# Attention scores: norms beside the up projections, paired score products, padded rotated rows

## The reference, cut to what matters

```python
q_nope = rms_norm(q[..., :128], mla_q_g[:128])          # 4 heads, 192 = 128 + 64
q_pe   = apply_rope(rms_norm(q[..., 128:], mla_q_g[128:]), cos, sin)
k_nope = rms_norm(kv[..., :128], mla_k_g[:128])
k_pe   = apply_rope(rms_norm(kpe_raw, mla_k_g[128:]), cos, sin)   # one, shared by the heads
out_m  = causal_attention(([q_nope, q_pe],), ([k_nope, k_pe],), (1.0,), v_m, 192 ** -0.5)
# differential attention: 4 heads with two score matrices of 64 features each
out_d  = causal_attention((qd0, qd1), (kd0, kd1), (1.0, -lam), vd, 64 ** -0.5)
# causal_attention: scores + causal mask, softmax, (sum_i c_i p_i) @ v, per block of 128 queries
```

## Time and profile before

| what | us |
|---|---|
| median of three runs | 3252.24 |
| span of the profiled execution, first to last instruction | 3238.1 |
| median less span (start and end of a run, and another execution) | 14.1 |
| PE busy, share of the span | 3122.7, 96% |
| DVE busy | 2023.3, 62% |
| ACT busy | 1268.4, 39% |
| POOL busy | 788.4, 24% |
| attention steps 0 to 14 (first score product to the MLA transposes) | 70.5 |
| MLA transposes | 5.7 |
| steps 15 to 35 | 46.8 |

### The profile page before, as it was taken

One profiled execution on the slowest core, in us unless ns is written; L12 is line 12 of the kernel. 1 busy time (PEld: TensorE's weight loads), 2 busy tenths in 40 slices (PEclk: granted clock), 3 DMA queues, 4 the chain that ended last, 5 costly groups with the idle time before them and its releaser, 6 DMA issues.

```text
span 3238.1 us, 42699 instructions
## 1 busy us (share of the span) xinstructions
PE 3122.7 (96%) x16801; PEld 2703.6 (83%) x16801; DVE 2023.3 (62%) x3671; ACT 1268.4 (39%) x2154; POOL 788.4 (24%) x513
## 2 busy tenths in 40 slices
PE   8999999989999999999998989999999997999999
PEld 6769989878888888888786678999999996888887
DVE  5576565663232464333458555989879767787877
ACT  6364443343232434322334332335444453333332
POOL 1000010100000020000002100686776764343452
PEclk9999999989999999999998899999999998999999
DMA  4303221233332323333231022578888889999997
GB/s 126 105 29 104 60 68 51 72 110 99 98 98 97 115 94 91 92 99 97 83 96 47 1 66 79 180 268 294 295 283 328 280 313 360 349 347 343 335 344 267
DMA packets 234375, 539.36 MB, mean 167 GB/s; under 512 B 24816, under 2 KB 91632, under 8 KB 231104
## 3 DMA queue, kind: packets, MB, share of 16 engines
q1 hardware_dynamic: 196736, 400.27, 37.5%
q0 software_dynamic: 37440, 136.36, 11.5%
HBM read 484.10 MB, written 52.46 MB: 166 GB/s over the span
## 4 chain that ended last, share of the span: by engine, by line
PE 76%; DVE 12%; DMA 6%; ACT 2%; POOL 2%; issue 1%; SPq 0%; DVEq 0%; ACTq 0%
PE bank L382 22%; PE bank L385 15%; PE bank L2349 11%; PE bank L2780 9%; DMA gl<-acts 4%; PE bank L2508 3%; PE bank L1109 2%; PE bank L1119 2%; PE bank L1070 2%; PE bank L1058 2%; PE bank L1923 1%; DVE vsl L2827 1%; DMA eu<-in_peer_u 1%; POOL etl L2337 1%; PE bank L505 1%
## 5 line engine op out<-in xcount | busy, mean ns | idle before, releaser
L332 DVE TENSOR_TENSOR wl<-raw,wh 128x1024 fp32r<-128x1024 f32 (+2 forms) x241 | 296.7, 1234 | 644.4 <-ACT wh L317 644.2
L317 ACT CAST wh<-raw 128x1024 fp32r<-128x1024 f32 (+2 forms) x241 | 249.7, 1038 | 655.8 <-PE bank L382 367.2
L2337 POOL TENSOR_TENSOR etl<-eu,eth 128x1024 fp32r<-128x1024 f32 x128 | 319.5, 2498 | 410.3 <-ACT eth L2333 408.9
L2349 PE MATMUL bank<-peerhh,eth 128*128 128x384 f32 x1024 | 349.6, 341 | 14.7 <-POOL etl L2337 12.6
L2349 PE MATMUL bank<-peerhl,eth 128*128 128x384 f32 x1024 | 344.0, 336 | 0.0
L2349 PE MATMUL bank<-peerhh,etl 128*128 128x384 f32 x1024 | 343.8, 336 | 0.0
L2780 PE MATMUL bank<-vsh,coefh 128*128 128x512 f32 x768 | 300.5, 391 | 19.2 <-DVE coefl L2847 19.2
L2374 POOL DMA_INDIRECT taken<-in_peer_v,gb x128 | 228.0, 1782 | 299.3 <-DVE y_row L2394 292.8
L2780 PE MATMUL bank<-vsh,coefl 128*128 128x512 f32 x768 | 299.8, 390 | 0.0
L2780 PE MATMUL bank<-vsl,coefh 128*128 128x512 f32 x768 | 299.8, 390 | 0.0
L2333 ACT CAST eth<-eu 128x1024 fp32r<-128x1024 f32 x128 | 135.7, 1061 | 200.1 <-DMA eu<-in_peer_u 195.5
(11 more groups left out here) (568 smaller groups left out, 7363.5 us busy)
## 6 DMA issues: line engine op xcount, KB each, us to landing
eu<-in_peer_u SPq DMA_DIRECT2D x128, 512.0 KB
vb<-in_peer_v SPq DMA_DIRECT2D x128, 512.0 KB, 5.6
raw<-in_ada_w SPq DMA_DIRECT2D x48, 512.0 KB, 3.8
acts<-eg SPq DMA_DIRECT2D x128, 192.0 KB
coefs<-stage SPq DMA_DIRECT2D x24, 1024.0 KB
gd<-coefs SPq DMA_DIRECT2D x16, 1536.0 KB, 12.9
gl<-acts SPq DMA_DIRECT2D x128, 192.0 KB
raw<-in_ffn_w_gate SPq DMA_DIRECT2D x44, 512.0 KB, 3.6
```

The source lines that it names most:

```text
L317: act.copy(parts_of(c)[0], raw_of(c)).then_inc(*up("w rounded", c))
L332: dve.tensor_tensor(lo, raw_of(c), hi.bitcast(F32), ALU.subtract).then_inc(*up("w split", c))
L2337: pool.tensor_tensor(Et[j % 3][1], Eu[j % 2], Et[j % 3][0].bitcast(F32), ALU.subtract).then_inc(*up("u split", j))
L2349: t = pe.matmul(b, tb[un][:, k * 128:(k + 1) * 128], peer_h[hn][:, k, 1:4, :], start=k == 0 and i == 0, stop=k == 7 and i == 2)
```

## The change

The squares and sums of the MLA queries move from steps 0 to 3 to the `kv up` projection and just behind it; the square of the shared rotated key moves into the latent squares; the squares and sums of the keys move to steps 4 to 7, their root to step 8, their scaling to steps 9 to 12. The shared key is rotated on POOL early, the queries after their own reciprocal. The small sums for lambda move before the latent norms. For a differential unit both score products are issued first, then both masks. `qp` and `kpe` get zeros in rows 64 to 127 (two memsets on POOL), and the product over them uses 128 rows.

The diff, cut to its core:

```diff
@@ pe_attn
-                        terms = [[(dqk[64 * s:64 * s + 64, hh, :], dqk[64 * s:64 * s + 64, 4 + hh, :])]
-                                 for s in range(2)]
+                        terms = [[(dqk[64 * s:64 * s + 64, hh, :], dqk[64 * s:64 * s + 64, 4 + hh, :], s)
+                                  for s in range(2)]]
-                        terms = [[(qn[:, hh, :], kn[:, hh, :]), (qp[0:64, hh, :], kpe[0:64, :])]]
+                        terms = [[(qn[:, hh, :], kn[:, hh, :], 0)], [(qp[:, hh, :], kpe, 0)]]
...
+                    for x, term in enumerate(terms):
+                        for l_, r__, s in term:
+                            pe.matmul(got[s][0][:, 0:n], l_[:, qt * 128:(qt + 1) * 128], r__[:, 0:n], start=x == 0,
                                       stop=False, skip_group_check=True)
+                    for i, (b, _) in zip(soft_ids(u), got):
                         pe.matmul(b[:, n - 128:n], ident, negm, start=False, stop=True,
@@ act_attn
+                    t = act.activation(wm[:, 1024 * tt + 640:1024 * tt + 704], pj[:, tt, 640:704], ACT.Square,
+                                       accum_out=rs[:, tt, 2:3])
...
+        evac_gemm("T", "kv up", cast, copier(0, act.copy, on_act, "kv up", kv),
+                  lambda n: q_squares(2 * n))
+        for tt in (1, 3):
+            q_squares(tt)
...
+            if 4 <= step < 8:
+                k_squares(step - 4)
+            if step == 8:
+                on_act.wait_ge(*at("dve step", "mla k", "mean"))
+                act.sqrt(rs[:, :, 12:16], rs[:, :, 12:16]).then_inc(*up("act root", "mla k"))
@@ dve_attn
+        evac_gemm("T", "kv up", rest, copier(1, dve.tensor_copy, on_dve, "kv up", kv),
+                  lambda n: q_sums(0) if n == 1 else None)
+        for tt in (2, 1, 3):
+            q_sums(tt)
...
+            if 4 <= step < 8:
+                k_sums(step - 4)
...
+            if 9 <= step < 13:
+                tt = step - 9
@@ pool_attn
+            rope(pool, on_pool, kp, 1, tt, rs[:, tt, 2:3], gmk, wm[:, 3584:4096], "pool step", ("rope", tt, 1))
+        on_pool.wait_ge(*at("tile full", "kv up", 1, 3))
...
+        pool.memset(qp[64:128], 0.0).then_inc(*up("rope rows zero", 0))
...
+        on_pool.wait_ge(*at("dve step", "mla q", "rstd"))
```

More of the change, by code:

```diff
@@ L2008, in act_attn @@
             act.copy(dqk[:, ft, :], banks["dqk", ft]).then_inc(*up("copied act", "dqk", ft))
[L2010 to L2020, removed]
-        for step in range(36):
[L2023 to L2027, removed]
+        on_act.wait_ge(*at("dve step", "mla q", "mean"))
+        act.sqrt(rs[:, :, 4:12], rs[:, :, 4:12]).then_inc(*up("act root", "mla q"))
+        on_act.wait_ge(*at("dve step", "lam", "sums"))
+        act.activation(ls[:, 0:2], ls[:, 0:2], ACT.Exp).then_inc(*up("lam exp"))
+        for step in range(36):
+            if 4 <= step < 8:
[3 more added lines that the diff above has]
+                act.sqrt(rs[:, :, 12:16], rs[:, :, 12:16]).then_inc(*up("act root", "mla k"))
             if step == 15:
@@ L2100, in dve_attn, with q_sums, k_sums @@
                   rope_beside(dve_rope_diff, dve, on_dve, "q up"))
[L2101 to L2106, removed]
+        def q_sums(tt):
+            j4 = mla_junk(tt).rearrange("p (h n) -> p h n", h=4)
+            on_dve.wait_ge(*at("q squares", tt))
+            dve.tensor_reduce(rs[:, tt, 4:8], j4[:, :, 0:128], AX.X, ALU.add)
+            dve.tensor_reduce(rs[:, tt, 8:12], j4[:, :, 128:192], AX.X, ALU.add).then_inc(*up("q sums", tt))
+        def k_sums(tt):
+            on_dve.wait_ge(*at("k squares", tt))
+            dve.tensor_reduce(rs[:, tt, 12:16], k_junk, AX.X, ALU.add).then_inc(*up("k sums", tt))
+        evac_gemm("T", "kv up", rest, copier(1, dve.tensor_copy, on_dve, "kv up", kv),
+                  lambda n: q_sums(0) if n == 1 else None)
+        for tt in (2, 1, 3):
+            q_sums(tt)
+        on_dve.wait_ge(*at("q sums", 3))
+        dve.tensor_scalar(rs[:, :, 4:8], rs[:, :, 4:8], 1.0 / 128, 1e-6, ALU.mult, ALU.add)
+        dve.tensor_scalar(rs[:, :, 8:12], rs[:, :, 8:12], 1.0 / 64, 1e-6, ALU.mult,
+                          ALU.add).then_inc(*up("dve step", "mla q", "mean"))
+        for ft in range(1, 8, 2):
+            on_dve.wait_ge(*at("bank full", "dqk", ft))
+            dve.tensor_copy(dqk[:, ft, :], banks["dqk", ft]).then_inc(*up("copied dve", "dqk", ft))
+        on_dve.wait_ge(*at("act root", "mla q"))
+        dve.reciprocal(rs[:, :, 4:12], rs[:, :, 4:12]).then_inc(*up("dve step", "mla q", "rstd"))
         on_dve.wait_ge(*at("lam exp"))
@@ L2111, in dve_attn @@
         on_dve.wait_ge(*at("dve step", "lam", "lam"))
[L2112 to L2132, removed]
@@ L2134, in dve_attn @@
         for step in range(36):
[L2135 to L2138, removed]
             if 4 <= step < 8:
-                tt = step - 4
+                k_sums(step - 4)
+            if step == 8:
+                on_dve.wait_ge(*at("k sums", 3))
+                dve.tensor_scalar(rs[:, :, 12:16], rs[:, :, 12:16], 1.0 / 128, 1e-6, ALU.mult,
+                                  ALU.add).then_inc(*up("dve step", "mla k", "mean"))
+                on_dve.wait_ge(*at("act root", "mla k"))
+                dve.reciprocal(rs[:, :, 12:16], rs[:, :, 12:16]).then_inc(*up("dve step", "mla k", "rstd"))
```

66 lines of the change are left out of this document (41 added, 25 removed).

## The result

The changed kernel took 3222.03 us (median of four, 3212.40 to 3224.14), the kernel before 3250.36 (median of four). The ratio is 0.9908, 95% interval 0.9889 to 0.9927: 30 us by the ratio, 28.3 by the medians. The direction was forecast; the size, 22.7, was too small. The forecast was counted from 3252.24, the median of three of these four runs of the kernel before.

A forecast was written before the change was run, and what follows sets the result against it. PE was busy 96%; the ACT and DVE chain bounded steps 0 to 3, the low clock steps 4 to 11. Gains 17.1 + 6.7 - 1.1 = 22.7 took 3252.2 to 3229.5 us, range 3222 to 3238.

The forecast's parts named there:

- steps 0 to 3: First attention steps: squares, sums and root leave the ACT and DVE chain; 6.2 us, to 1753.4, gain 9.4.
- steps 4 to 7: Attention steps taking over the keys' squares and sums, with waits for ACT; 16.5 us against 16.2, gain -0.3.
- steps 8 to 14: Attention up to the MLA transposes: paired products, clock back by about step 9 or 10; 27.0 us, to 1796.9.
- steps 15 to 35: MLA units, PE-bound at full clock, 46.8 us before: each loses two row changes, 0.4; gain 6.7 in sum.
- latents: Latent norms ahead of attention: the shared key's square lengthens PE's wait; cost 1.1 us, bounds 0.8 and 2.5.
- Rival 2: No fall of the clock in attention: steps 9 to 14 take 21, not 22.1; 3227; chance 0.70 shared with forecast.
- Rival 1: Low clock lasts until the MLA transposes: 3237 with products side by side, 3244 in turn; chance 0.15.
- The memsets: POOL's zeroing, 5 us at most, fits before the queries' reciprocal at 1746.7; cost 0.
- the POOL rotation: About 24 us of rotation on POOL ends by 1771 to 1776, some 20 before the transposes need it; cost 0.
- the squares beside `kv up`: Four squares of 0.74 us each fit ACT's gaps of 2 to 3 there; cost 0, bounds 0 and 1.5.

The follow-up runs named there:

- same half twice: Kernel before with both score products issued side by side, but both reading rows 0 to 63; 3239.2 us, one run.
- by 128 rows: Kernel before in its old order (product, mask, product, mask), each differential product over all 128 rows; 3227.3 us, one run.
- norms and padding in turn: Changed kernel with product, mask, product, mask again in a differential unit; 3240.0 us, ratio 0.9975.
- Norms alone: Changed kernel without issuing score products side by side and without zero rows, so only the norms moved; 3246.1 us, ratio 0.9980.
- pairs alone: Kernel before with only a differential unit's two score products issued side by side, then both masks; 3224.8 us, ratio 0.9930.
- padding alone: Kernel before with only `qp` and `kpe` zeroed in rows 64 to 127 and 128 rows in their product; 3242.6 us, ratio 0.9986.

## Why the forecast was right and wrong

From the input projections to the attention's output product the profile gained 26.6, where 22.7 were forecast:

| step of the sum | forecast | measured |
|---|---|---|
| steps 0 to 3, with the start behind `kv up` | 9.4 | 9.5 |
| steps 4 to 7 | -0.3 | -0.1 |
| steps 8 to 14 | 8.0 | 11.8 |
| steps 15 to 35 and the tail | 6.7 | 8.1 |
| latents | -1.1 | -2.7 |

*The step that failed: steps 8 to 14*, with what was to bring the clock back in them. The forecast had the clock back by about step 9 or 10, because PE would follow product on product with fewer pauses for row changes, and 27.0 us for these steps. Measured are 11.8 of gain instead of 8.0, for two reasons. The clock was back at step 8, so DVE ended step 14 25.4 us after step 7's end. And I equated that end with the start of the transposes; PE issued these 2.35 before it (1798.17 against 1800.52), since they don't wait for the last units' outputs. Rival 2 (no fall at all) asked for 21 us in steps 9 to 14: 20.7 were measured, with two falls ahead of them.

The reason given for the clock was wrong, and not only its size. The kernel with the same half twice has exactly these fewer changes of rows, and its clock stayed low for 41.0 us; what brought it back early was that all rows were at work, by pairs (17.1) or by 128 rows (10.2). The forecast also let the clock fall for PE's pauses, and it falls without them (norms and padding in turn).

*Luck in the sum.* The terms of steps 0 to 3 and 8 to 14 are not additive, and the forecast didn't see it. It gave 9.4 of the gain to steps 0 to 3, that is to the norms. Norms alone gave 3.3, since the low clock simply moved on to dearer steps; the pairs alone gave 19.2 with steps 0 to 3 unchanged. With the clock back early the stretch runs at DVE's and ACT's pace, and then the norms are worth 3.2, less the 3.9 that they cost ahead. Rival 1 (low clock to the transposes) is what the change would have been without the pairs: its 3244 stands beside 3240.0 for norms and padding in turn. Had the forecast asked which part ends the low clock, its range would have rested on one edit. The transposes' start at 1798.17, where 1798 was forecast, is luck as well: all was 2.7 later from the input projections on.

*Steps 0 to 3 and 4 to 7* went as priced: DVE took 8.7 us from the first score product to the end of step 3 (its last output starts at 1758.57), less 1.1 later start behind `kv up`, then 16.3 with four waits of 0.99. The memsets, the POOL rotation and the squares beside `kv up` were covered, as forecast.

*Steps 15 to 35*: 40.6 us against 46.8, so 6.2 of the 6.7; padding alone gave 5.7. The other 1.9 is mostly the spell of low clock in the tail of the earlier trace rows, which this execution lacked. *Latents*: the wait grew to 2.32 as forecast (near 2), which is 1.2; but the clock fell behind it (1693.7 to 1697.1), which I had left out, and that added 1.5, in both profiles of the changed kernel. The 2.7 lie outside the bounds of 0.8 and 2.5.

*Slips in the working.* The costs named for a step with n = 128 add to 1.86 with the output; 1.63 holds without it, and so the sum used it. The named bounds add to gains of 13.8 to 28.0, that is 3224 to 3238; the 3222 at the lower end has 2 more in it than they give, and the measured 3222.03 lies there. The chances named for "faster by more" add to 0.85, not 0.86.

## What to carry to other kernels

Where a stretch runs at the low clock with PE always busy, don't look only for the pause ahead of its fall: look at what PE does in it. In this one stretch half-row products in turn went with 41 to 51 us at 0.50, all rows at work with spells of 3 to 17, and two products from both halves next to each other were worth more than any work taken off the other engines. And price parts of a change against each other, one alone and one left out: a gain that only moves the low clock to later, dearer steps is given back.

## What the hardware showed

- Products of 64 rows from both halves overlap fully: 1.06 for a pair of 512 columns, 1.05 for one; from one half, two of 512 columns take 1.91.
- A product over 128 rows, half of them zero, is cheaper than one over 64 among products of 128: 0.86 against 1.05 at 512 columns.
- The clock stayed at 0.50 for 47.8 us with PE busy throughout on half-row products in turn, and was back after 3.4 and 6.8 us with PE as busy on pairs from both halves.
- The clock fell without a pause of PE of more than 0.3 us ahead of it, while half-row products ran in turn.
- More work on PE made the stretch shorter in the profiled executions: 16 score products doubled, 44.1 to 41.9, with one fall of the clock fewer. The medians, 3217.5 and 3213.5, don't tell the two apart.
- POOL writes 64x2048 zeros in 1.80 us and 64x512 in 0.52.
